# Decays of a chunked state-space scan as differences of running sums

## The reference, cut to what matters

```python
a_cs = jnp.cumsum(jnp.moveaxis(dt * a, 2, -1), axis=-1)
tri = idx[:, None] >= idx[None, :]
seg = a_cs[..., :, None] - a_cs[..., None, :]
decay = jnp.exp(jnp.where(tri, seg, -jnp.inf))
cb = jnp.einsum("bclgn,bcsgn->bcgls", cm, bm)
y_diag = jnp.einsum("bcgrls,bcsgrp->bclgrp", cb[:, :, :, None] * decay, xdt)
```

## Time and profile before

| | us |
|---|---|
| median of 3 runs | 1990.78 |
| lowest, highest | 1989.66, 1991.36 |
| the profiled execution, its time | 1989.5 |
| the profiled execution, its span | 1987.8 |
| PE busy in the span | 1940.4 (98%) |
| DVE, ACT, POOL busy | 735.4, 650.9, 496.4 |

### The profile page before, as it was taken

One profiled execution on the slowest core, in us unless ns is written; L12 is line 12 of the kernel. 1 busy time (PEld: TensorE's weight loads), 2 busy tenths in 40 slices (PEclk: granted clock), 3 DMA queues, 4 the chain that ended last, 5 costly groups with the idle time before them and its releaser, 6 DMA issues.

```text
span 1987.8 us, 28733 instructions
## 1 busy us (share of the span) xinstructions
PE 1940.4 (98%) x11839; PEld 1704.8 (86%) x11839; DVE 735.4 (37%) x1076; ACT 650.9 (33%) x1069; POOL 496.4 (25%) x263
## 2 busy tenths in 40 slices
PE   7999999999999999999999999999999999999996
PEld 7887778888888887877679999999999999888885
DVE  5624564210010005856732000010000101999996
ACT  4332222232222224356630000000000001888883
POOL 3546664265445543442121000000000000000010
PEclk9999999999999999999999999999999999999998
DMA  7962222233333332320009878879787887999995
GB/s 254 313 202 64 69 80 85 75 118 95 100 101 96 96 103 71 110 85 22 33 1 381 291 251 287 294 277 319 278 314 282 291 305 279 382 377 387 367 413 211
DMA packets 295103, 405.38 MB, mean 204 GB/s; under 512 B 11272, under 2 KB 211034, under 8 KB 294970
## 3 DMA queue, kind: packets, MB, share of 16 engines
q1 hardware_dynamic: 292666, 395.12, 57.0%
q0 software_dynamic: 2304, 8.39, 1.1%
HBM read 372.67 MB, written 30.80 MB: 203 GB/s over the span
## 4 chain that ended last, share of the span: by engine, by line
PE 90%; issue 3%; DVE 2%; POOL 2%; ACT 1%; SPq 0%; DVEq 0%; POOLq 0%; DMA 0%; ACTq 0%
PE ps L1999 21%; PE ps L2006 10%; PE ps L399 6%; PE ps L401 6%; PE ps L400 6%; PE ps L2060 5%; PE ps L2062 5%; PE ps L2061 5%; PE ps L417 3%; PE ps L419 3%; PE ps L418 3%; PE ps L547 2%; PE ps L549 2%; PE ps L548 2%; PE ps L435 1%
## 5 line engine op out<-in xcount | busy, mean ns | idle before, releaser
L1242 POOL TENSOR_TENSOR w_lo<-raw,w_hi 128x1024 fp32r<-128x1024 f32 (+1 forms) x159 | 387.9, 2449 | 351.0 <-ACT w_hi L935 350.8
L1846 DVE TENSOR_TENSOR s_lo<-s_raw,s_hi 128x1024 fp32r<-128x1024 f32 x198 | 235.3, 1222 | 22.2 <-ACT s_hi L2206 13.8
L2448 DVE TENSOR_TENSOR hid<-ps,silu_g 128x160 f32<-128x160 f32 x110 | 35.7, 325 | 542.9 <-ACT silu_g L2181 542.9
L935 ACT ACTIVATE w_hi<-raw 128x1024 fp32r<-128x1024 f32 (+1 forms) x159 | 164.8, 1044 | 193.9 <-PE ps L419 115.8
L399 PE MATMUL ps<-act_a_hi,w_hi 128*128 128x512 f32 x568 | 226.3, 398 | 0.0
L2181 ACT ACTIVATE silu_g<-ps 128x160 f32<-128x160 f32 x110 | 33.4, 303 | 585.9 <-PE ps L1999 585.9
L1999 PE MATMUL ps<-xT,w_up 128*128 128x132 f32 (+1 forms) x1760 | 224.2, 281 | 0.0
L1999 PE MATMUL ps<-xT,w_gate 128*128 128x132 f32 (+1 forms) x1760 | 224.2, 281 | 0.0
L401 PE MATMUL ps<-act_a_hi,w_lo 128*128 128x512 f32 x568 | 221.2, 389 | 0.0
L400 PE MATMUL ps<-act_a_lo,w_hi 128*128 128x512 f32 x568 | 221.2, 389 | 0.0
L2206 ACT ACTIVATE s_hi<-s_raw 128x1024 fp32r<-128x1024 f32 x198 | 205.6, 1059 | 42.7 <-PE ps L2062 37.1
(11 more groups left out here) (369 smaller groups left out, 2909.5 us busy)
## 6 DMA issues: line engine op xcount, KB each, us to landing
w_gate<-in_moe_w_gate SPq DMA_DIRECT2D x55, 1024.0 KB, 5.2
w_up<-in_moe_w_up SPq DMA_DIRECT2D x55, 1024.0 KB, 8.3
w_down<-in_moe_w_down SPq DMA_DIRECT2D x55, 1024.0 KB, 10.5
s_raw<-in_moe_w_gate SPq DMA_DIRECT2D x33, 1024.0 KB, 7.8
s_raw<-in_moe_w_up SPq DMA_DIRECT2D x33, 1024.0 KB, 7.9
s_raw<-in_moe_w_down SPq DMA_DIRECT2D x33, 1024.0 KB, 7.7
raw<-in_even_w_in SPq DMA_DIRECT2D x43, 512.0 KB, 5.2
raw<-in_attn_w_qkv SPq DMA_DIRECT2D x24, 512.0 KB, 3.7
```

The source lines that it names most:

```text
L935: act.activation(w_hi[:, u % HL_SLOTS, 0:size(u)], raw[:, u % RAW_SLOTS, 0:size(u)], ACT.Copy).then_inc(hi_done, 1)
L1242: pool.tensor_tensor(w_lo[:, u % HL_SLOTS, 0:size(u)], raw[:, u % RAW_SLOTS, 0:size(u)], flat(w_hi[:, u % HL_SLOTS, 0:size(u)]), ALU.subtr ...
L1846: return eng.tensor_tensor(s_lo[u % S_HL][:], s_raw[u // 2 % S_RAW][:, u % 2, :], s_hi[u % S_HL][:].bitcast(F32), ALU.subtract)
```

## The change

The differences are no longer made of log decays by an fp32 product with a triangle. Instead:

- DVE copies the log decays four times over beside each other, with gaps (`logs_again`, in `conv_in`). In the last unit of the second gate group, ahead of its third tile, PE multiplies them with `t_incl` (four fp32 products of 128 x 128, `running_sums`): the running sums of each head then lie along the free axis, turned, in bank 3.
- DVE makes two operands of them, `sum_from` and `sum_to` (in `act_b_hi[:, 7]` and `act_b_lo[:, 7]`, which the convolution branch fills last), each rounded to a part that fp32r keeps and the rest in another block of partitions, with rows that pick a head and rows that put a large negative number where `tri` is false. This takes 20 DVE instructions more.
- A piece of four heads is now one fp32r product of `sum_from` (of the chunk) and `spans`, which POOL makes of `sum_to` and the choice of heads.
- ACT's exponentials for `dt` move from behind the second gate group to behind the first.
- In POOL's `ssd_first` the log decays of pieces 2 and 3 stand ahead of the wait for `es_ready` and of `xw`.
- `weigh` is a scalar_tensor_tensor that also takes the minimum with 1; the last one of a chunk stands between the first and the second tap of the convolution.
- DVE clears all of `conv_in` at the start; POOL makes two rows of numbers there.

The diff, without semaphore names and comments:

```diff
@@ tiles @@
-    dtri, o = place("dtri", [P, 2, 4, P], F32, o)
+    spans, o = place("spans", [P, 2, 4, P], F32R, o)
+    sum_from, sum_to = act_b_hi[:, KD - 1, :], act_b_lo[:, KD - 1, :]
+    own_head, logs_again = dts[:, 7, 0:SSD_HEADS], conv_in[:, 8:8 + SEQ]
@@ PE @@
-        pe.wait_ge(dt_abs, 1)
-        token_out(G_Z + 1, U_Z + 4, KD, of(act_a_hi, act_a_lo))
+        pe.wait_ge(dt_made, 1)
+        def running_sums(i, tile):
+            if (i, tile) == (3, 2):
+                pe.wait_ge(z_evac, NT)
+                pe.wait_ge(dt_made, 2)
+                for c in range(NT):
+                    d = logs_again[:, c * P:(c + 1) * P]
+                    mm = pe.matmul(ps[:, 3, c * P:(c + 1) * P], d, t_incl[:], start=True, stop=True)
+                mm.then_inc(sums_done, 1)
+        token_out(G_Z + 1, U_Z + 4, KD, of(act_a_hi, act_a_lo), running_sums)
...
-            pe.matmul(ps[:, 6 + h % 2, :], t_gt[:], dtri[:, h % 2].rearrange("p a b -> p (a b)"),
+            pe.matmul(ps[:, 6 + h % 2, :], sum_from[:, c * P:(c + 1) * P], spans[:, h % 2].rearrange("p a b -> p (a b)"),
@@ ACT, gate groups g = 0, 1 @@
-        act.wait_ge(dt_abs, 1)
-        act.activation(dts[:, 3, :], dts[:, 2, :], ACT.Exp, scale=-1.0)
-        act.activation(small[:, 48:64], small[:, 16:32], ACT.Exp).then_inc(dt_exp, 1)
+            if g == 0:
+                act.wait_ge(dt_made, 1)
+                act.activation(dts[:, 3, :], dts[:, 2, :], ACT.Exp, scale=-1.0)
+                act.activation(small[:, 48:64], small[:, 16:32], ACT.Exp).then_inc(dt_exp, 1)
@@ POOL @@
                                heads(dts[:, 0], c * 16, 16), ALU.mult).then_inc(xdt_ready, 1)
+            log_decays(c, 2)
+            log_decays(c, 3)
             pool.wait_ge(es_ready, c + 1)
             pool.drain()
             pool.tensor_tensor(xw[:].rearrange("p (h d) -> p h d", h=SSD_HEADS),
...
-            log_decays(c, 2)
-            log_decays(c, 3)
...
-            pool.tensor_tensor(dtri[:, h % 2], t_incl[:].unsqueeze(1).to_broadcast([P, 4, P]),
-                               d.unsqueeze(2).to_broadcast([P, 4, P]), ALU.mult).then_inc(dtri_ready, 1)
+            pool.tensor_tensor(spans[:, h % 2], sum_to[:, c * P:(c + 1) * P].unsqueeze(1).to_broadcast([P, 4, P]),
+                               own_head[:, 4 * h:4 * h + 4].unsqueeze(2).to_broadcast([P, 4, P]), ALU.mult).then_inc(spans_ready, 1)
@@ DVE, behind the log decays @@
-                                 ALU.mult).then_inc(dt_ready, 1)
+                                 ALU.mult)
+        dve.drain()
+        dve.tensor_copy(logs_again.rearrange("p (t q h) -> p t q h", t=NT, q=4)[:, :, :, 0:16],
+                        dts[:, 1, :].rearrange("p (t h) -> p t h", t=NT).unsqueeze(2).to_broadcast([P, NT, 4, 16])
+                        ).then_inc(dt_made, 1)
...
+        dve.tensor_scalar(sum_from[half, :].rearrange("p (t l) -> p t l", t=NT),
+                          upto[half, :].unsqueeze(1).to_broadcast([64, NT, P]), chosen[half, :], None, ALU.add)
+        dve.wait_ge(sums_done, 1)
+        dve.tensor_copy(sum_to, ps[:, 3, :])
+        dve.drain()
+        dve.tensor_scalar(sum_from[0:32, :], sum_to[0:32, :], -1.0, None, ALU.mult)
+        dve.tensor_tensor(sum_from[32:64, :], sum_to[32:64, :], ps[32:64, 3, :], ALU.subtract)
+        dve.tensor_tensor(sum_to[96:P, :], ps[96:P, 3, :], sum_to[96:P, :], ALU.subtract)
+        dve.drain()
+        dve.memset(sum_to[0:64, :].bitcast(F32), 1.0)
+        s_tl = sum_to[half, :].rearrange("p (t l) -> p t l", t=NT)
+        dve.tensor_tensor(s_tl, s_tl, below[half, :].unsqueeze(1).to_broadcast([64, NT, P]), ALU.add)
+        dve.drain().then_inc(dt_made, 1)
@@ DVE, weigh @@
-            dve.tensor_tensor(m, m, cbm[:, h // 2, :].unsqueeze(1).to_broadcast([P, 4, P]),
-                              ALU.mult).then_inc(mix_ready, 1)
+            dve.scalar_tensor_tensor(m, m, 1.0, cbm[:, h // 2, :].unsqueeze(1).to_broadcast([P, 4, P]),
+                                     ALU.min, ALU.mult).then_inc(mix_ready, 1)
@@ DVE, the convolution @@
             dve.tensor_scalar(conv_acc, conv_in[:, 0:512], w[0], None, ALU.mult)
+            if a % 2:
+                weigh(a // 2, 3)
             for j in (1, 2):
                 dve.drain()
                 dve.scalar_tensor_tensor(conv_acc, conv_in[:, j:j + 512], w[j], conv_acc, ALU.mult, ALU.add)
-            if a % 2:
-                weigh(a // 2, 3)
```

More of the change, by code:

```diff
@@ L211, in build_trunk @@
     xbc_evac, xbc_conv, xbc_silu = sem("xbc_evac"), sem("xbc_conv"), sem("xbc_silu")
-    dt_evac, dt_turned, dt_abs, dt_exp, dt_ready = (sem("dt_evac"), sem("dt_turned"), sem("dt_abs"),
-                                                    sem("dt_exp"), sem("dt_ready"))
+    dt_evac, dt_turned, dt_exp = sem("dt_evac"), sem("dt_turned"), sem("dt_exp")
+    dt_made = sem("dt_made")
     z_evac = sem("z_evac")
+    sums_done = sem("sums_done")
     cg_evac, cghv_ready, bg_used, ya_hi, ya_lo = (sem("cg_evac"), sem("cghv_ready"), sem("bg_used"),
@@ L676, in ssd_first @@
                 pe.wait_ge(z_evac, 2 * NT)
-                pe.wait_ge(dt_ready, 1)
+                pe.wait_ge(dt_made, 3)
             for f in range(KD):
@@ L1254, in _ @@
         pool.memset(mix[:, 0:D // P, :], 0.0)
+        pool.iota(state[:, 0:P], [[1, P]], base=0, channel_multiplier=0, allow_small_or_imprecise_dtypes=True)
+        pool.iota(state[:, 384:385], [[0, 1]], base=0, channel_multiplier=4, allow_small_or_imprecise_dtypes=True)
         pool.drain().then_inc(zero_ready, 1)
@@ L1291, in _ @@
         pool.wait_ge(small_in, 48)
-        pool.wait_ge(dt_ready, 1)
+        pool.wait_ge(dt_made, 3)
         for a in range(KD):
@@ L1418, in _ @@
         dve.memset(xbc_in[:, :, 0:3], 0.0)
-        dve.memset(conv_in[:, 0:2], 0.0)
+        dve.memset(conv_in[:], 0.0)
         dve.drain().then_inc(pads_ready, 1)
@@ L1465, in _ @@
                                  small[:, 48:64].unsqueeze(1).to_broadcast([P, NT, 16]), ALU.mult,
-                                 ALU.mult).then_inc(dt_ready, 1)
+                                 ALU.mult)
[3 more added lines that the diff above has]
+                        ).then_inc(dt_made, 1)
+        number, below, upto, four_p, chosen, rest, first, past = (state[:, 0:P], state[:, P:2 * P], state[:, 2 * P:3 * P],
+                                                                  *(state[:, 384 + i:385 + i] for i in range(5)))
@@ new lines, in _ @@
+        half = slice(64, P)
+        dve.wait_ge(zero_ready, 1)
+        dve.reduce_sum(own_head, ident[:].rearrange("p (q r) -> p r q", q=4)[:, 0:SSD_HEADS, :], AX.X)
+        dve.tensor_scalar(first[64:96, :], four_p[64:96, :], -320.0, None, ALU.add)
+        dve.tensor_scalar(first[96:P, :], four_p[96:P, :], -384.0, None, ALU.add)
+        dve.drain()
+        dve.reduce_sum(chosen, own_head, AX.X)
+        dve.drain()
+        dve.tensor_scalar(rest, chosen, -1.0, 1.0, ALU.mult, ALU.add)
+        dve.drain()
@@ new lines, in _ @@
+        dve.tensor_scalar(own_head, own_head, rest, None, ALU.add)
+        dve.tensor_tensor(first[half, :], first[half, :], rest[half, :], ALU.mult)
+        dve.drain()
+        dve.tensor_scalar(past[half, :], first[half, :], 4.0, None, ALU.add)
+        dve.tensor_scalar(below[half, :], number[half, :], first[half, :], None, ALU.is_lt)
+        dve.drain()
+        dve.tensor_scalar(upto[half, :], number[half, :], past[half, :], rest[half, :], ALU.is_lt, ALU.mult)
+        dve.drain()
+        dve.tensor_tensor(upto[half, :], upto[half, :], below[half, :], ALU.subtract)
@@ new lines, in _ @@
+        dve.tensor_scalar(below[half, :], below[half, :], -65536.0, None, ALU.mult)
+        dve.drain()
+        dve.tensor_scalar(sum_from[half, :].rearrange("p (t l) -> p t l", t=NT),
+                          upto[half, :].unsqueeze(1).to_broadcast([64, NT, P]), chosen[half, :], None, ALU.add)
+        dve.wait_ge(sums_done, 1)
+        dve.tensor_copy(sum_to, ps[:, 3, :])
+        dve.drain()
+        dve.tensor_scalar(sum_from[0:32, :], sum_to[0:32, :], -1.0, None, ALU.mult)
+        dve.tensor_tensor(sum_from[32:64, :], sum_to[32:64, :], ps[32:64, 3, :], ALU.subtract)
```

7 lines of the change are left out of this document (3 added, 4 removed).

## The result

The changed kernel took 1977.7 us (median of 4 runs, 1976.0 to 1979.6) where the kernel before took 1991.0 beside it (4 runs, 1989.7 to 1991.4): ratio 0.9937, interval 0.9926 to 0.9949, 13.3 us less. The forecast was 1979.0 with a range of 1976.3 to 1983.3. The profiled execution took 1975.96 us, its span 1974.2.

The account below looks back on a forecast made before the run. PE was taken to bound the convolution and scan stretch. Decay products -9.7, stalls -3.1 and running sums +1.0 made -11.8 us, from a median of 1990.8 to 1979.0; range for 8 in 10: 1976.3 to 1983.3.

Parts of the forecast that it names:

- Terms 1 and 2: Scan's decay products as fp32r: eight between units save 0.63 us each, four chunk heads 1.16 each, 9.7 in all.
- Term 3: PE's three stalls for POOL's log decays in the scan go with `spans` ahead of `xw`: 3.1 us, bounds 0 to 3.4.
- rival 1: Scan stalls stay, DVE slipping in or another POOL chain link late: 1982.1 us; 15% for 1981 to 1983.5, 4% beyond.
- The SBUF rule in the forecast: A `weigh` could slip in between `xdt` and `spans`, costing 0.68 us at chunks 2 and 3; stall gain then 2.1.
- Term 4: The four fp32 products of the running sums, late in the gate, add 1.0 us on PE.
- a sign of being wrong: PE waiting ahead of `running_sums` or `ssd_second`, or the 12 us there at 310 us and gone at the end.
- The series on DVE: DVE's log decay steps, moved into the gate: 5.0 us, copy at about 113, 10 us of slack, cost 0.
- Rival 4: PE waits in the gate for the copied log decays or at chunk 0 for `sum_from`: 1991 us and more; 3%.
- The fourth `weigh`'s move: Between the convolution's taps on DVE, it uses time in which DVE would otherwise reach the taps: cost 0.
- ACT's table loads: Extra loads of 1.28 us around the moved exponentials in the gate: cost 0, up to 1.3 us each without cover.
- rival 2: The new decay product keeps two passes and does not stream like the projections: only 2.1 us less, 1988.7; 3%.
- Rival 3: `weigh` in its new form takes twice 0.68 us, adds 11 us and makes DVE the bound: 1990.0 us; 2%.

Follow-up runs that it names:

- experiment 2: Changed kernel with the 16 decay products in fp32 in place of fp32r: 1987.4 us, ratio 0.9987.
- experiment 1: Kernel before with one edit, POOL's log decays of pieces 2 and 3 ahead of `xw`: 1987.5 us, ratio 0.9986.
- experiment 3: Changed kernel with `xw` ahead of the log decays of pieces 2 and 3 on POOL again: 1984.9 us, ratio 0.9969.
- Experiment 7: Changed kernel with the four products of the running sums one unit earlier in the gate: 1980.3 us, ratio 0.9950.
- experiment 4: Changed kernel with the last `weigh` of a chunk behind the two taps of the convolution again: 1981.3 us, ratio 0.9953.
- experiment 6: Changed kernel with `weigh` as tensor_tensor, without the minimum with 1: 1976.4 us, ratio 0.9928.
- the second set: Later set of runs, with the changed kernel unedited once more (1978.4 us, ratio 0.9939) against the kernel before (1990.6 us).
- experiment 8: Changed kernel with the last `weigh` of a chunk ahead of the first tap of the convolution: 1976.5 us, ratio 0.9931.

## Why the prediction was right, step by step

**What bounds the kernel.** Right. Everything that left PE's stream left the time: 12.07 us at the first product behind the scan, and none of it was given back; the rest is no longer than before (1680.0 and 1681.5).

**Terms 1 and 2 (9.7 us): right.** Eight distances went from 1.32 to 0.68, 0.64 each, 5.1 together (5.0 forecast). The heads of the chunks save 2.05 - 0.80 = 1.25 each, 5.0 together (4.6 forecast): I had the first fp32r product behind fp32 ones at 0.43, and it took 0.34. A last 0.4 is outside my two distances: at chunk 1 the first decay product stood 19.98 us ahead of the first product of `ssd_second` (190.00 and 209.98) and now stands 17.36 ahead of it (186.74 and 204.10), 2.62 less where one head and two distances give 2.53. The projections behind an fp32 decay product started up to 0.01 us further apart than 0.227, and now don't. That makes 10.5 in all, as in experiment 2, so the two terms were 0.8 too small.

**Term 3 (3.1 us): right in size, partly wrong in cause.** The three stalls of 3.4 us are gone, and one wait of 0.36 is new, so 3.0. POOL's order does it, shown from both sides (experiments 1 and 3). At chunk 0 I let up to 0.5 stand and none did. With the old order it lost 1.61 before and 0.56 in experiment 3, so the early `dt` helps there as the forecast has it, but with the new order the kernel before needed no such help (experiment 1). Chunk 3 was said to be clear and isn't. POOL there, and DVE:

```profile
274.47 1.90 POOL L1285 TENSOR_TENSOR xdt<-xs,dts 128x1024 f32<-128x1024 f32 x1
276.33 2.93 POOL L1298 TENSOR_TENSOR spans<-act_b_lo,dts 128x512 fp32r<-128x512 f32 x2
```

```profile
274.98 3.38 DVE L1540 SCALAR_TENSOR_TENSOR mix<-mix,cbm 128x512 f32<-128x512 f32 x2
```

The pair of `spans` takes 2.93 where an undisturbed pair takes 2.04 (two `dtri` in the earlier trace rows did too): two `weigh`s stood beside `xdt` and got in between. This is rival 1's mechanism, in its small form: a `weigh` does slip in, and costs 0.36 once, because the relief covers most of it. The SBUF rule in the forecast gave 0.5 at chunk 2 and at chunk 3; it is right on what happens and high on the price. Chunk 2 has the same 2.95 for its pair and shows no wait. What differs is when the chain gets there: `spans` starts 4.23 us behind the chunk's first decay product at chunk 2 and 4.73 at chunk 3. The chain that ended last leads back to two DVE instructions in `ssd_second` of chunk 2, beside POOL's `xw`:

```profile
253.00 1.91 POOL L1303 TENSOR_TENSOR xw<-xs,small 128x1024 f32<-128x1024 f32 x1
```

```profile
253.68 2.47 DVE L1562 TENSOR_TENSOR state<-state,es 64x512 f32<-64x512 f32 x2
```

A chunk earlier these two took 1.99, with `xw` 1.2 us ahead of them and not 0.7. That half us is the one by which `spans` is later. Either delay alone, this one or some 0.45 us that the `weigh` costs the first of the pair, would by these numbers have left no wait; this is worked out and not run.

**Term 4 (+1.0): right.** 0.9 us (gate 43.99 to 44.89; eight records, 0.89 on the chain).

**The sum.** In the scan -5.1 - 5.0 - 0.4 - 3.0 + 0.5 (two new waits for `weigh`) = -13.0, as measured. With the gate -12.1, -11.8 forecast. The hit is closer than its parts, and that is luck: the kind of product gave 0.8 more than forecast, and two waits that I had priced at nothing took 0.5 of it back. They are also what I had named as a sign of being wrong: PE waits ahead of `ssd_second`, for 0.28 and 0.20 us, too little to overturn the sum.

**What I put at nothing.** Three steps; one was that, one was it by luck, one was not.

- The series on DVE: forecast 5.0 us, ending at 112.6 with the copy at 113. Measured 107.70 to 118.79, 11.1 us, and the copy at 119.15. Its single instructions of 64 columns, and POOL beside them:

```profile
108.59 0.23 DVE L1465 TENSOR_TENSOR dts<-dts 128x64 f32<-128x64 f32 x1
108.89 2.28 DVE L1467 TENSOR_TENSOR dts<-dts 128x64 f32<-128x64 f32 x1
111.25 2.24 DVE L1469 TENSOR_SCALAR dts<-dts 128x64 f32<-128x64 f32 x1
...
116.23 2.26 DVE L1478 SCALAR_TENSOR_TENSOR dts<-dts 128x64 f32<-128x64 f32 x1
...
118.86 0.29 DVE L1484 COPY conv_in<-dts 128x256 f32<-128x256 f32 x1
```

```profile
108.69 4.75 POOL L1258 TENSOR_TENSOR w_lo<-raw,w_hi 128x1024 fp32r<-128x1024 f32 x2 [6.61 <-ACT w_hi L951]
...
116.00 2.41 POOL L1258 TENSOR_TENSOR w_lo<-raw,w_hi 128x1024 fp32r<-128x1024 f32 x1 [2.56 <-ACT w_hi L951]
```

Three steps of 0.2 us took 2.24 to 2.28, each nearly as long as the one `w_lo` beside it (2.4). The old place of the series, at 129 to 134 us, was one where POOL idled; my 5.0 us were read there and carried to a place where it works. The Trainium skill ("SBUF — State Buffer", section "Who interferes with whom") states that exclusion for the whole of an instruction, and I had used it for `weigh` and not here: by it, each `w_lo` that starts within the series adds its 2.4. The trace agrees: with three of them the series is 6.1 us longer. One of the three steps, L1469, has a single tile as its input. The longer series cost no time, because 3.6 us of slack were left. The operands behind the sums were ready at 128.7 (128 to 137 forecast), POOL's first `spans` began at 128.85 (129), and PE asked for them at 145.5. Experiment 7 shows the edge of it. Rival 4 had this place and needed the copy 22 us late; it came 6 us later than forecast.

- The fourth `weigh`'s move: not nothing but about 3 us, the largest thing I left out, hidden in the forecast since the kernel before had no wait there. With a PE that comes 0.6 us earlier at each product, behind the taps it is too late (experiment 4). At the new place it still waits for POOL's `w_lo`, and PE for it:

```profile
238.23 7.75 POOL L1258 TENSOR_TENSOR w_lo<-raw,w_hi 128x1024 fp32r<-128x1024 f32 x3
```

```profile
241.71 2.01 DVE L1584 TENSOR_SCALAR htmp<-conv_in,cols 128x512 f32<-128x512 f32 x1
243.64 2.88 DVE L1540 SCALAR_TENSOR_TENSOR mix<-mix,cbm 128x512 f32<-128x512 f32 x1
```

0.68 us of work, 2.88 of record, and L727 starts at 246.57, 0.40 behind the last projection product, where 0.23 is the step. I had asked whether the move made another instruction late and not who would wait if it were left where it was.

- ACT's table loads: right, nothing. SiLU's came back while ACT had nothing to do, ahead of group 2:

```profile
121.38 1.28 ACT L1042 ACT_TABLE_LOAD   x1
...
126.59 2.07 ACT L1042 ACTIVATE zs<-ps 128x512 f32<-128x512 f32 x4 [3.93 <-PE ps L424]
```

**The other rivals.** Rival 1 in full would have left some of the three stalls, and did not. The product streams like its neighbours, so rival 2 falls; experiment 2 is what it would have been, 1987.4 (priced 1988.7). What the forecast calls two passes are two records. Rival 3 falls by experiment 6, rival 4 by the gate's 44.89.

**The 1.5 us behind the scan** are not the change's. The kernel before was granted less in one place of its profiled execution, 990 to 1010 us, the changed one was not:

```profile
990.00:1000.00 10.00, 8.25 (x38) 6.21 (x37) 3.51 (x6) 5.41 (x10) 2.87 (x3) 0.95 0.00 0
1000.00:1010.00 10.00, 10.00 (x41) 8.15 (x40) 2.71 (x2) 2.12 (x2) 8.04 (x5) 0.88 0.00 0
```

```profile
980.00:990.00 10.00, 8.27 (x38) 6.22 (x37) 3.84 (x7) 6.22 (x9) 4.88 (x4) 1.00 0.00 0
990.00:1000.00 10.00, 10.00 (x46) 8.28 (x45) 1.91 (x2) 0.79 (x2) 6.06 (x4) 1.00 0.00 0
```

The changed kernel is at the same work 12 us earlier: PE idles for 1.56 us ahead of L630 before, from 996.6 us on, and for 1.57 ahead of L635 now, from 984.6 on, and only the first was followed by a lower clock. The missing shares, 0.5 and 1.2, are 1.7 us. The rests of the eight experiments lie between 1680.1 and 1681.8. By gate and scan the change is worth 12.1 us, and the second set's 12.3 (1990.6 and 1978.4) agrees.

## What to carry to other kernels

Where one engine bounds a stretch, forecast by the distances between its starts at the places that change, at a clean place and at a switch between kinds of product, and add the stalls from the same rows. Then ask of every other engine's instruction that feeds it two things: how late it is if the bounding engine comes earlier, and how long its record is beside the work that now runs next to it; a duration read where the neighbour idled (5.0 us) can be twice as long elsewhere (11.1). A small step that is moved "for free" may be what keeps the gain: undo it alone before calling it nothing.

## What the runs showed of the hardware that was not expected

**A short idle time of PE can cost more than itself.** Behind a wait of 1.88 us at 237 to 239 us (experiment 3) the granted clock was 0.83 for ten us, 1.7 us more; in experiment 4 two such stretches, behind waits of about 0.9 and 1.9 us, cost up to 3.4 each. In all ten profiles each drop of the clock ahead of the last 20 us stands in an idle time of PE or shortly behind one. It does not follow every one: experiment 3 waited as long again at chunk 3 without a drop, and the kernel before lost 1.6 us near 153 us and 0.9 near 243 with a clock of 1.00 over the whole stretch. Nor does the length decide alone: 1.56 and 1.57 us at the same work, above, went both ways. What decides it these runs don't show.

**The same kernel starts in one of two ways.** PE idles for a moment at 20 us while data come in. In five of the ten profiles (before, changed, experiments 2, 6 and 8) the clock from 20 to 25 us was 1.00 and the gate began at 81.35 to 81.50 us; in the other five it was 0.66 or 0.71 and the gate began at 82.82 to 82.96. PE's idle time at 20 us was 1.45 to 1.68 us in the first five and 1.92 to 2.65 in the others, with the same end (21.3 to 21.5 us). The code up to there is the same but for small instructions on DVE and POOL, and the changed kernel was seen in both. These 1.5 us and those of the places above are as large as what one tries to measure: runs of the kernel before with a mean clock of 0.995 took 1989.3 to 1990.2 but for two of 1990.8, at 0.994 mostly 1990.6 to 1991.5.

**Short DVE instructions pay a whole POOL instruction**: 0.23 us alone, 2.28 beside a `w_lo` of 2.4, three times in one series.
